# Twenty row sums moved behind the dense tiles' picks in a hybrid layer with product-key experts

## The chip, the cores and the metric

The kernel runs on one core of one Trainium2 chip, in float32. The metric is device time in microseconds of one execution; lower is better. "Before" has a median of 1618.62 us over three runs (1617.82 to 1620.2).

## What is computed

One layer over 512 tokens of width 1024: a token-mixing sublayer (windowed attention and an HGRN2 recurrence, merged by gates, projected, layer norm) and then the part that this case is about, a PEER layer that picks 16 experts of 16384 for each of 8 heads and each token:

```python
def block(xt):                                   # 128 tokens
    q = (xt @ wq).reshape(128, 8, 2, 128)
    s1 = einsum('thd,kd->thk', q[:, :, 0], keys[0]);  s2 = ... keys[1]
    v1, i1 = top_k(s1, 16);  v2, i2 = top_k(s2, 16)
    cand = v1[..., :, None] + v2[..., None, :]   # 256 sums
    sc, ci = top_k(cand, 16)
    e = i1[ci // 16] * 128 + i2[ci % 16]         # expert number
    g = softmax(sc)
    act = gelu(einsum('thkd,td->thk', u[e], xt))
    return einsum('thk,thkd->td', g * act, v[e])
x = layer_norm(ALPHA * x + mix(x));  x = layer_norm(ALPHA * x + peer(x))
```

`u` is the first table and `v` the second, 16384 rows of 1024 each.

## The kernel before

The tokens are four tiles of 128. Tile 0 goes through the mixing sublayer alone (`A`), tiles 1 to 3 together (`B`). Then PEER is done in two ways.

**Tiles 0 and 1 gather.** For each of the 128 picks (8 heads x 16) of a token tile, GpSimd fetches 128 rows of 4 KB (0.524 MB) by an indirect DMA into one of 12 slots, and VectorE handles this "row": for `u` a product with x summed up (L1181), for `v` a scaled addition to the result (L1196). There are 512 such rows: 0 to 127 are `u` for tile 0, 128 to 255 `v` for tile 0, 256 to 383 `u` for tile 1, 384 to 511 `v` for tile 1. GpSimd refills a pair of slots once VectorE has used them. A hand-written plan says how many rows VectorE has done at each place of its program (`rows_until`). VectorE's instructions run in the order written, so a row in front of a step delays the step.

**Tiles 2 and 3 are dense.** They go through both tables in whole. A first-table block c is 128 experts: TensorE multiplies a `u` block of 0.524 MB with both tiles (L855, 16 records), ScalarE applies gelu, `act[c]` stays on chip or is spilled to `act_d`. There are 128 such blocks and TensorE starts them as soon as `B` is projected. Four `u` buffers: SyncE asks for block c's when block c - 4 is done. Meanwhile VectorE routes tile 1 (four pairs of heads) and tiles 2 and 3 (two halves each), with rows between the steps. Then come the "picks": normalised gates and expert halves, turned by TensorE (L864), copied by ScalarE. In between, at block `TURN_AT`, TensorE waits for them (`pick_ready`). From them VectorE makes 64 one-hot pairs (`one_hots`, L1504 and L1506), with `HOT_ROWS` rows spread over them, and TensorE multiplies each pair (`spread`, four matrix products, L873), which gives the gates of four tokens for all 16384 experts, a "gate product" below. `quads_by` says after which block which one is due. ScalarE copies them, and six groups of eight go to memory (`gates_d`); the last two stay on chip.

In the second table, block i of `act` is multiplied by its gates on VectorE (`weigh`, L1521 and L1522), which waits for its slice of eight blocks of gates (`load_gates`), and TensorE adds its product with a `v` block (`combine`, L879, 8 records). VectorE's remaining rows are spread over this table by `rows_at`, then tile 1's norm. At the very end the norms of tiles 2 and 3 follow.

SyncE issues nearly all loads in one order, waiting as written. Before, after the last `u` load:

```python
            sp.wait_ge(pick_ready, len(DENSE))
            for i in range(2):
                load_v(i)
            for k in range(2):
                sp.wait_ge(g_stored[k], 16 * (STORED // 2))
            load_gates(0)
            sp.wait_ge(g_done, QUADS)
```

The second slice, `load_gates(1)`, takes the place of the first table's input and so is asked for after the last block of it.

Of the kernel before, what the change touches and what calls it, by code (L numbers as in the profile page):

```python
# [36 lines left out]
NE = PH * TOPK  # L37
# [25 lines left out]
DENSE = (2, 3)  # L63
ND = len(DENSE) * P
EXPERTS = NK
# [3 lines left out]
FIRST = SPILL + RINGED_ACT  # L69
# [4 lines left out]
STORED = GROUPS - 2  # L74
# [1 line left out]
QUADS = ND // QUAD  # L76
GBLK = 8
EXP1_AT = 24
EXP_AT = 50
TURN_AT = 52  # L80
SPREAD_AT, SPREAD_END = 53, 116
ROOT0_Q = 44
GELU1_AT = 112
PAIR = 2
EARLY_ROWS, PAIR_ROWS, HALF_ROWS = 204, 7, 8
HOT_ROWS = 104
MID_ROWS = 390
ACT_BACK_LEAD = 12


# [9 lines left out]

def rows_at(i):

    return min(4 * NE, MID_ROWS + int(3.2 * min(i, EXPERTS - FIRST)) + int(1.0 * max(0, i - EXPERTS + FIRST)))


NORM1_W = min(i for i in range(EXPERTS) if rows_at(i) == 4 * NE)
# [77 lines left out]
def build(nc, x, xT, w_items, keysT, pos, inv_freq, sinks, lb_logits, norm_g,  # L184
          ln1, ln2, ident_d, causal_d, chunk_d, iota_d, u_rows, v_rows, u_cols, v_cols, gates_d, act_d, out):
    with ExitStack() as ctx:
# [253 lines left out]
        def _(sp):  # L440
# [54 lines left out]
            def load_v(i):  # L495

                if i >= VBUFS:
                    sp.wait_ge(o_done, i - VBUFS + 1)
                sp.dma_start(v_buf[i % VBUFS], v_cols[chunk(i)]).then_inc(v_in[i % VBUFS], 16)

            def load_gates(b):

                if b >= 2:
                    sp.wait_ge(w_ready, GBLK * (b - 1))
                src = gates_d.rearrange("g p (b n) -> b p g n", b=EXPERTS // GBLK)
                sp.dma_start(g_buf[b % 2].rearrange("p g c t -> p g (c t)"), src[chunk(b * GBLK) // GBLK]
                             ).then_inc(g_in[b % 2], 16)
# [19 lines left out]
            for c in range(EXPERTS):  # L527
                load_u(c)
                b, late = divmod(c - BATCH - UBUFS, BATCH)
                if late == 0 and 0 <= b < SPILL // BATCH:  # L530
                    spill(b)
            sp.wait_ge(pick_ready, len(DENSE))
            for i in range(2):
                load_v(i)
            for k in range(2):
                sp.wait_ge(g_stored[k], 16 * (STORED // 2))
            load_gates(0)
            sp.wait_ge(g_done, QUADS)
            for i in range(2, 4):
                load_v(i)  # L540
# [591 lines left out]
        def _(dve):  # L1132
# [38 lines left out]
            def rows_until(q):  # L1171

                while done[0] < q:
                    r = done[0]
                    s, t, k = r % SLOTS, r // (2 * NE), r % NE
                    if r % (2 * NE) < NE:
                        if t and k == NE // 2:
                            dve.wait_ge(row_used, r)
                            dve.sem_inc(hid_ready, 1)
                        dve.wait_ge(landed[s // 2], 32 * (r // SLOTS + 1))  # L1180
                        v.tensor_tensor_reduce(rows[:, s, :], rows[:, s, :], x1[:, t, :], 1.0, 0.0,  # L1181
                                               ALU.mult, ALU.add, hid[:, k:k + 1]).then_inc(row_used, 1)
                    else:
                        if k == 0:
                            dve.wait_ge(row_used, r)
                            dve.sem_inc(hid_ready, 1)
                            dve.wait_ge(gexp_done, t + 1)
                            normalise(gexp)
                            weights(t + 1, slice(0, NE // 2 if t else NE))
                            steps(lambda: v.tensor_scalar(acc[t], x1[:, t, :], ALPHA, None, ALU.mult))  # L1190
                        if t and k == NE // 2:
                            weights(t + 2, slice(NE // 2, NE))
                        dve.wait_ge(landed[s // 2], 32 * (r // SLOTS + 1))

                        dve.wait_ge(row_used, r)
                        v.scalar_tensor_tensor(out=acc[t], in0=rows[:, s, :], scalar=wv[:, k:k + 1], in1=acc[t],  # L1196
                                               op0=ALU.mult, op1=ALU.add).then_inc(row_used, 1)
                    done[0] += 1
# [296 lines left out]
            def one_hots(d, first):  # L1495

                dve.wait_ge(pick_out, 2 * (d + 1))
                for q in range(d * QUADS // len(DENSE), (d + 1) * QUADS // len(DENSE)):
                    if q >= 2:
                        dve.wait_ge(g_done, q - 1)  # L1500
                    ts = slice(q * QUAD - d * P, (q + 1) * QUAD - d * P)
                    both = [P, 2, QUAD, NK]
                    out = hot[:, q % 2, :, :].rearrange("p (k j) e -> p k j e", k=2)
                    steps(lambda: v.tensor_tensor(out, iota[:, :].unsqueeze(1).unsqueeze(1).to_broadcast(both),  # L1504
                                                  idxT[d][:, :, ts].unsqueeze(3).to_broadcast(both), ALU.is_equal))
                    v.tensor_tensor(out[:, 1, :, :], out[:, 1, :, :],  # L1506
                                    gT[d][:, ts].unsqueeze(2).to_broadcast([P, QUAD, NK]), ALU.mult).then_inc(hot_ready, 1)
                    rows_until(first + HOT_ROWS * (q + 1) // QUADS)

# [74 lines left out]
                gate_args(d)  # L1584
            for d in range(len(DENSE)):
                gate_weights(d)
            rows_until(2 * NE)
            dve.wait_ge(row_used, 2 * NE)
            dve.wait_ge(ln_in, 64)
            dve.sem_inc(route_gate, 1)  # L1590
            one_hots(0, first)
            both_stats(acc[0])
            one_hots(1, first)
            norm_scale(0, acc[0], std2_ready, y2_ready)
# [89 lines left out]
```

## Time and profile before

| | us |
|---|---|
| Median of three runs | 1618.62 |
| Profiled execution | 1628.27 |
| Its span | 1626.5 |
| TensorE (PE) busy | 1540.3, 95% |
| VectorE (DVE) busy | 1130.7, 70% |
| GpSimd (POOL) busy | 623.7, 38% |
| ScalarE (ACT) busy | 273.8, 17% |
| Mixing and projections, TensorE | 0 to 650.0 |
| First table, TensorE | 652.8 to 1168.3 |
| Second table, TensorE | 1177.1 to 1619.2 |

The queues moved 532.39 MB, 327 GB/s over the span. A float32 matrix product stands in the trace as two records. Times in the trace are of the profiled execution, which is 9.65 us longer than the median of the others.

### The profile page before, as it was taken

How to read it: one execution, taken by the hardware profiler on the slowest of the kernel's cores; microseconds unless marked ns; L12 is line 12 of the kernel's file. 1: busy time of each engine (PE TensorE's matmuls, PEld its weight loads, DVE VectorE, ACT ScalarE, POOL GpSimd, SP SyncE). 2: the span in 40 equal slices, each digit the busy share in tenths (PEclk: the TensorE clock that was granted, in tenths of full speed). 3: DMA queues.
4: the chain of work that ended last, by engine and by line, in shares of the span. 5: the costliest groups of instructions: out<-in, count | busy, mean ns of one | idle time of the engine just before them, and what ended most of it. 6: DMA issues, size and time to landing. Idle time of an engine off the chain costs nothing.

```text
span 1626.5 us, 18100 instructions
## 1 busy us (share of the span) xinstructions
PE 1540.3 (95%) x6542; PEld 1098.4 (68%) x6542; DVE 1130.7 (70%) x2492; ACT 273.8 (17%) x543; POOL 623.7 (38%) x516
## 2 busy tenths in 40 slices
PE   7798799869999899999979999999799999999998
PEld 7697568755557666888869999999644444444443
DVE  1413889877778989999998888889574544444442
ACT  2601111731010112111113333433100000000000
POOL 0001533455676473323225555555543323323200
PEclk9898899878999999999989999999999999999999
DMA  7586958757999898998879999999999999999952
GB/s 290 208 280 220 401 167 298 258 191 243 414 388 374 309 413 332 320 344 302 328 250 338 405 415 411 405 381 324 392 403 392 381 374 369 376 371 376 363 199 90
DMA packets 142856, 532.39 MB, mean 327 GB/s; under 512 B 15024, under 2 KB 30128, under 8 KB 130480
## 3 DMA queue, kind: packets, MB, share of 16 engines
q0 software_dynamic: 73728, 268.47, 44.2%
q1 hardware_dynamic: 68176, 250.19, 41.0%
q10 hardware_dynamic: 864, 12.58, 1.8%
q8 instruction: 52, 0.85, 0.2%
q14 instruction: 36, 0.29, 0.0%
HBM read 503.92 MB, written 27.26 MB: 327 GB/s over the span
## 4 chain that ended last, share of the span: by engine, by line
PE 71%; DVE 15%; issue 6%; DMA 3%; ACT 2%; POOL 1%; SPq 1%; another core or an unknown queue 0%; DVEq 0%
PE bank L879 27%; PE bank L855 15%; PE bank L749 7%; PE bank L596 4%; PE bank L873 4%; DVE arena L1196 3%; PE bank L584 3%; DVE arena L1401 2%; PE bank L835 2%; DVE arena L1397 2%; PE bank L759 2%; PE bank L761 2%; POOL arena L1619 1%; PE bank L780 1%; DVE arena L1406 1%
## 5 line engine op out<-in xcount | busy, mean ns | idle before, releaser
L1619 POOL DMA_INDIRECT arena<-u_d,arena x256 | 341.6, 1334 | 496.9 <-DVE arena L1181 253.8
L855 PE MATMUL bank<-arena 128*128 128x256 f32 x2048 | 456.8, 381 | 2.7 <-DMA arena<-u_cols_d 2.7
L879 PE MATMUL bank<-arena 128*128 128x512 f32 x1024 | 442.1, 595 | 8.8 <-DVE arena L1522 8.8
L1619 POOL DMA_INDIRECT arena<-v_d,arena x256 | 281.9, 1101 | 404.9 <-DVE arena L1196 345.3
L855 PEld LDWEIGHTS bank<-arena 128*128 128x128 f32 x2048 | 387.0, 192 | 53.6 <-issue 2.9
L879 PEld LDWEIGHTS bank<-arena 128*128 128x128 f32 x1024 | 195.4, 191 | 255.0 <-issue 243.9
L1196 DVE SCALAR_TENSOR_TENSOR arena<-arena 128x1024 f32<-128x1024 f32 x256 | 327.5, 1279 | 13.0 <-DMA arena<-v_d,arena 3.6
L1181 DVE CUSTOM_DVE_ANT_0 arena<-arena 128x1024 f32<-128x1024 f32 x256 | 303.2, 1219 | 12.1 <-DMA arena<-u_d,arena 11.7
L1521 DVE TENSOR_TENSOR arena<-arena 128x192 f32<-128x192 f32 x128 | 45.0, 352 | 208.3 <-DMA arena<-act_d 167.4
L835 PE MATMUL bank<-arena 128*128 128x128 f32 (+1 forms) x512 | 124.0, 401 | 9.7 <-issue 7.8
L835 PEld LDWEIGHTS bank<-arena 128*128 128x128 f32 x512 | 84.8, 208 | 45.6 <-issue 12.0
L749 PE MATMUL bank<-arena 128*128 128x128 f32 (+1 forms) x512 | 114.4, 385 | 0.0
L1074 ACT ACTIVATE arena<-bank 128x256 f32<-128x256 f32 x128 | 49.0, 384 | 343.0 <-PE bank L855 332.0
L749 PEld LDWEIGHTS bank<-arena 128*128 128x128 f32 x512 | 78.3, 193 | 35.0 <-issue 2.0
L596 PE MATMUL bank<-arena 128*128 128x256 f32 x448 | 98.7, 383 | 0.0
L596 PEld LDWEIGHTS bank<-arena 128*128 128x128 f32 x448 | 85.7, 192 | 12.3 <-issue 0.2
L1102 ACT ACTIVATE rstd<-rstd 128x1 f32<-128x1 f32 x4 | 0.8, 202 | 450.7 <-DVE rstd L1377 450.6
L1093 ACT ACTIVATE arena<-bank 128x512 f32<-128x512 f32 x64 | 69.1, 1082 | 31.5 <-PE bank L873 28.4
L873 PEld LDWEIGHTS bank<-arena 128*128 128x128 f32 x512 | 67.1, 192 | 3.3
L873 PE MATMUL bank<-arena 128*128 128x128 f32 x512 | 67.3, 275 | 0.0
L584 PE MATMUL bank<-arena 128*128 128x128 f32 (+1 forms) x256 | 57.9, 390 | 8.5 <-DMA arena<-w_items_d 8.5
L584 PEld LDWEIGHTS bank<-arena 128*128 128x128 f32 x256 | 40.4, 200 | 25.4 <-issue 7.5
(199 smaller groups left out, 1115.7 us busy)
## 6 DMA issues: line engine op xcount, KB each, us to landing
arena<-w_items_d SPq DMA_DIRECT2D x66, 1024.0 KB, 8.7
arena<-u_cols_d SPq DMA_DIRECT2D x128, 512.0 KB
arena<-v_cols_d SPq DMA_DIRECT2D x128, 512.0 KB
act_d<-arena SPq DMA_DIRECT2D x12, 1024.0 KB, 10.3
gates_d<-arena ACTq DMA_DIRECT2D x6, 2048.0 KB
arena<-gates_d SPq DMA_DIRECT2D x16, 768.0 KB, 10.1
arena<-act_d SPq DMA_DIRECT2D x12, 1024.0 KB, 12.3
arena<-u_d,arena POOLq DMA_INDIRECT x256
```

The costliest lines, as they stand in the source:

```text
L584: last = mm(bank[:, b % 4, 0:n], w[:, c, b % 2 * P:(b % 2 + 1) * P], F.act_in[:, c, :], start=c == 0, stop=c == KC - 1)
L596: last = mm(bank[:, b % 4, 0:TW], F.act_in[:, c, t * P:(t + 1) * P], w[:, c, :], start=c == 0, stop=c == KC - 1)
L749: last = mm(bank[:, b + g, 0:n], w[:, g * KC + c, :], F.act_in[:, c, :], start=c == 0, stop=c == KC - 1)
L835: last = mm(bank[:, b % 4, 0:n], w[:, c, half * P:(half + 1) * P], F.act_in[:, c, :], start=c == 0, stop=c == KC - 1)
L855: last = mm(bank[:, 4 + c % 2, 0:ND], u_buf[:, c % UBUFS, k, :], B.act_in[:, k, B.n - ND:B.n], start=k == 0, stop=k == KC - 1)
L873: last = mm(bank[:, 6 + q % 2, j * NK:(j + 1) * NK], hot[:, q % 2, j, :], hot[:, q % 2, QUAD + j, :], start=True, stop=True)
L879: return mm(bank[:, 2 * n + half, :], act_slot(i)[:, n * P:(n + 1) * P], v_buf[i % VBUFS][:, half * 512:(half + 1) * 512], start=i == 0, s ...
L1074: fn(act_ring[c % RINGED_ACT], bank[:, 4 + c % 2, 0:ND], ACT.Gelu).then_inc(act_done, 1)
L1093: fn(stage[g % 2][:, :, k * QUAD:(k + 1) * QUAD].rearrange("p e t -> p t e"), bank[:, 6 + q % 2, :].rearrange("p (t e) -> p t e", t=QUAD), ...
L1181: v.tensor_tensor_reduce(rows[:, s, :], rows[:, s, :], x1[:, t, :], 1.0, 0.0, ALU.mult, ALU.add, hid[:, k:k + 1]).then_inc(row_used, 1)
L1196: v.scalar_tensor_tensor(out=acc[t], in0=rows[:, s, :], scalar=wv[:, k:k + 1], in1=acc[t], op0=ALU.mult, op1=ALU.add).then_inc(row_used, 1)
L1619: pool.indirect_dma_start(rows[:, r % SLOTS, :], None, table, bass.IndirectOffsetOnAxis(eidx[:, t, k:k + 1], 0)).then_inc(landed[r % SLOTS ...
```

## The change

Six numbers of the plan, two places in SyncE's order and one in VectorE's.

```diff
-EXP_AT = 50
-TURN_AT = 52
-SPREAD_AT, SPREAD_END = 53, 116
+EXP_AT = 44
+TURN_AT = 46
+SPREAD_AT, SPREAD_END = 47, 118
+GATES_AT, VALUES_AT = 114, 118
-EARLY_ROWS, PAIR_ROWS, HALF_ROWS = 204, 7, 8
-HOT_ROWS = 104
-MID_ROWS = 390
+EARLY_ROWS, PAIR_ROWS, HALF_ROWS = 192, 6, 7
+HOT_ROWS = 126
+MID_ROWS = 374
 ...
-    return min(4 * NE, MID_ROWS + int(3.2 * min(i, EXPERTS - FIRST)) + int(1.0 * max(0, i - EXPERTS + FIRST)))
+    return min(4 * NE, MID_ROWS + int(3.2 * min(i, EXPERTS - FIRST)) + int(1.1 * max(0, i - EXPERTS + FIRST)))
 ...
                     spill(b)
-            sp.wait_ge(pick_ready, len(DENSE))
-            for i in range(2):
-                load_v(i)
-            for k in range(2):
-                sp.wait_ge(g_stored[k], 16 * (STORED // 2))
-            load_gates(0)
+                if c == GATES_AT:
+                    sp.wait_ge(pick_ready, len(DENSE))
+                    for k in range(2):
+                        sp.wait_ge(g_stored[k], 16 * (STORED // 2))
+                    load_gates(0)
+                if c == VALUES_AT:
+                    for i in range(2):
+                        load_v(i)
             sp.wait_ge(g_done, QUADS)
 ...
                 gate_weights(d)
-            rows_until(2 * NE)
+            one_hots(0, first)
+            assert done[0] >= 2 * NE
             dve.wait_ge(row_used, 2 * NE)
             dve.wait_ge(ln_in, 64)
             dve.sem_inc(route_gate, 1)
-            one_hots(0, first)
             both_stats(acc[0])
```

Rows done at each place, worked out from these numbers:

| Place in VectorE's program | before | after |
|---|---|---|
| start of tile 1's routing | 204 | 192 |
| after tile 1's four pairs | 232 | 216 |
| after the four halves, at the picks | 264 | 244 |
| after the 64 one-hot pairs | 368 | 370 |
| before block 0 is weighed | 390 | 374 |
| all 512, at block | 122 | 126 |

(SPREAD_AT and SPREAD_END give the blocks: 64 gate products over 63 blocks before, over 71 after.) With 244 rows at the picks, tile 0 (256 rows) is not finished there, so the wait for its last row moves behind the first 32 one-hot pairs, just ahead of its statistics.

What stands in a row on VectorE between the end of `B`'s norms and the first steps of tile 1's routing (L1196 is a value row, L1397 the first maximum of the routing), before:

```order
L1384 RECIPROCAL rstd<-rstd 128x1
L1387 SCALAR_TENSOR_TENSOR arena<-arena,rstd 128x512 x2
L1196 SCALAR_TENSOR_TENSOR arena<-arena 128x1024 x44
L1397 MAX arena<-arena 128x8 x4
L1401 MAX_INDEX arena<-arena 128x8 x4
L1406 MATCH_REPLACE arena<-arena 128x128 x4
```

and after (lines are three further down):

```order
L1387 RECIPROCAL rstd<-rstd 128x1
L1390 SCALAR_TENSOR_TENSOR arena<-arena,rstd 128x512 x2
L1199 SCALAR_TENSOR_TENSOR arena<-arena 128x1024 x32
L1400 MAX arena<-arena 128x8 x4
L1404 MAX_INDEX arena<-arena 128x8 x4
L1409 MATCH_REPLACE arena<-arena 128x128 x4
```

Twelve value rows have left this place.

TensorE from the last key scores over the first-table blocks (eight matrix products each) to the picks and the first gate products, before:

```order
L823 MATMUL bank<-keys,arena 128x128 x12
L855 MATMUL bank<-arena 128x256 x416
L864 MATMUL bank<-ident,arena 128x128 x3
L864 MATMUL bank<-ident,state_in 128x128 x2
L864 MATMUL bank<-ident,arena 128x128
L855 MATMUL bank<-arena 128x256 x16
L873 MATMUL bank<-arena 128x128 x4
L855 MATMUL bank<-arena 128x256 x8
```

and after:

```order
L826 MATMUL bank<-keys,arena 128x128 x12
L858 MATMUL bank<-arena 128x256 x368
L867 MATMUL bank<-ident,arena 128x128 x3
L867 MATMUL bank<-ident,state_in 128x128 x2
L867 MATMUL bank<-ident,arena 128x128
L858 MATMUL bank<-arena 128x256 x24
L876 MATMUL bank<-arena 128x128 x4
L858 MATMUL bank<-arena 128x256 x8
```

The picks stand after 46 blocks instead of 52, and three blocks instead of two lie between them and the first gate product.

SyncE's queue from the last spill (`act_d`) to the second gate slice, before:

```order
L514 DMA act_d<-arena 128x2048
L492 DMA arena<-u_cols_d 128x1024 x27
L499 DMA arena<-v_cols_d 128x1024 x2
L506 DMA arena<-gates_d 128x6x256
L499 DMA arena<-v_cols_d 128x1024 x6
L506 DMA arena<-gates_d 128x6x256
```

and after:

```order
L515 DMA act_d<-arena 128x2048
L493 DMA arena<-u_cols_d 128x1024 x14
L507 DMA arena<-gates_d 128x6x256
L493 DMA arena<-u_cols_d 128x1024 x4
L500 DMA arena<-v_cols_d 128x1024 x2
L493 DMA arena<-u_cols_d 128x1024 x9
L500 DMA arena<-v_cols_d 128x1024 x6
L507 DMA arena<-gates_d 128x6x256
```

The first slice stands ahead of the last thirteen `u` loads and the first two `v` blocks ahead of the last nine.

## Rows read from the trace of the kernel before

**Rows 1.** Page, part 1: busy us (share) xinstructions:

```profile
PE 1540.3 (95%) x6542; PEld 1098.4 (68%) x6542; DVE 1130.7 (70%) x2492; ACT 273.8 (17%) x543; POOL 623.7 (38%) x516
```

**Rows 2.** Timeline of PE at the first table; start us, us, line, xcount, [idle before]:

```profile
652.75 12.50 PE L855 MATMUL bank<-arena 128*128 128x256 f32 x49 [2.73 <-DMA arena<-u_cols_d]
...
809.70 24.55 PE L855 MATMUL bank<-arena 128*128 128x256 f32 x113
844.57 0.90 PE L864 MATMUL bank<-ident,arena 128*128 128x128 f32 x3 [10.32 <-DVEq L1493]
...
846.27 9.30 PE L855 MATMUL bank<-arena 128*128 128x256 f32 x32
855.40 1.05 PE L873 MATMUL bank<-arena 128*128 128x128 f32 x8
...
859.75 1.05 PE L873 MATMUL bank<-arena 128*128 128x128 f32 x8
```

**Rows 3.** Timeline of PE at the start of the second table:

```profile
1177.09 23.22 PE L879 MATMUL bank<-arena 128*128 128x512 f32 x48 [8.80 <-DVE arena L1522]
```

**Rows 4.** Stretches: us; busy (xcount) of PE, PEld, DVE, ACT, POOL; PEclk; DMA share; GB/s:

```profile
652.00:656.00 4.00, 3.25 (x8) 2.65 (x9) 3.51 (x9) 0.00 (x0) 1.51 (x3) 0.60 0.96 341
844.00:850.00 6.00, 5.33 (x15) 4.22 (x16) 4.68 (x10) 2.98 (x8) 1.64 (x2) 0.50 0.54 176
1177.00:1183.00 6.00, 5.91 (x9) 2.59 (x10) 6.00 (x13) 0.00 (x0) 2.19 (x2) 0.60 1.02 408
```

**Rows 5.** Timeline of DVE from the last norm to routing's pair 0:

```profile
552.09 44.34 DVE L1196 SCALAR_TENSOR_TENSOR arena<-arena 128x1024 f32<-128x1024 f32 x32
...
615.61 0.86 DVE L1397 MAX8 arena<-arena 128x8 f32<-128x128 f32 x4
...
636.92 1.28 DVE L1196 SCALAR_TENSOR_TENSOR arena<-arena 128x1024 f32<-128x1024 f32 x1
638.12 0.17 DVE L1572 CAST arena<-arena 128x32 uint32<-128x32 f32 x1
```

**Rows 6.** Timeline of ACT, head 3's scores copied:

```profile
618.21 0.38 ACT L1054 ACTIVATE arena<-bank 128x256 f32<-128x256 f32 x1 [0.28 <-remote]
```

**Rows 7.** Timeline of DVE, first step of tile 2's routing and tile 3's gate argument:

```profile
706.95 1.65 DVE L1397 MAX8 arena<-arena 128x8 f32<-128x128 f32 x8
...
843.41 0.29 DVE L1486 TENSOR_TENSOR arena<-arena 128x128 f32<-128x128 f32 x1
```

**Rows 8.** Timeline of DVE, one gate product with two row sums:

```profile
1121.64 1.22 DVE L1504 TENSOR_TENSOR arena<-iota,state_in 128x1024 f32<-128x1024 f32 x1
...
1123.51 1.22 DVE L1181 CUSTOM_DVE_ANT_0 arena<-arena 128x1024 f32<-128x1024 f32 x1
...
1125.80 1.28 DVE L1381 SCALAR_TENSOR_TENSOR arena<-arena,mv 128x1024 f32<-128x1024 f32 x1
```

**Rows 9.** Busy time by stretches; then PEclk, DMA share, GB/s:

```profile
888.00:1080.00 192.00, 192.00 (x1061) 173.73 (x1060) 168.79 (x238) 67.24 (x92) 103.44 (x72) 1.00 1.02 410
1190.00:1240.00 50.00, 50.00 (x118) 22.07 (x117) 25.78 (x48) 0.00 (x0) 17.22 (x16) 1.00 1.03 402
1250.00:1500.00 250.00, 250.00 (x584) 110.70 (x583) 119.16 (x223) 0.00 (x0) 80.23 (x75) 1.00 0.99 375
```

**Rows 10.** Timeline of the SP queue at the table change:

```profile
1156.61 0.38 SPq L506 DMA_DIRECT2D arena<-gates_d  x1
```

**Rows 11.** Timeline of DVE at the table change:

```profile
1176.54 0.36 DVE L1521 TENSOR_TENSOR arena<-arena 128x192 f32<-128x192 f32 x1 [14.85 <-DMA arena<-gates_d]
```

**Rows 12.** Gate values' transfers, to and from memory:

```profile
L1097 ACTq DMA_DIRECT2D gates_d<-arena x6: 326/326/347, 888.0 to 1061.9; - x6
...
DMA to landing us min/median/max: 5.5/10.1/28.6
```

**Rows 13.** Timeline of DVE at the end:

```profile
1608.91 0.69 DVE L1536 SCALAR_TENSOR_TENSOR arena<-arena,bank 128x512 f32<-128x512 f32 x1 [34.33 <-PE bank L879]
```

**Rows 14.** Timeline of PE at the end:

```profile
1579.53 39.65 PE L879 MATMUL bank<-arena 128*128 128x512 f32 x92
```

## The prediction, made before the changed kernel was run

> **What bounds the kernel now.** I read the page's busy shares first: TensorE is busy for 95% of the span [rows 1]. So the time is TensorE's work plus its few idle places, and I looked for these in its timeline. From the first table's start to the end there are three. It waits 2.73 us for the first `u` load. It stands 10.32 us ahead of the picks, after 52 of the 128 first-table blocks [rows 2]. It stands 8.80 us between the first and the second table [rows 3]. Each also costs time afterwards: the granted clock is 0.50 in the stretch after the picks, 0.60 in the stretch after the second gap and 0.60 after the first load [rows 4], that is, partly or wholly at 1.2 instead of 2.4 GHz. After the picks, two blocks take 9.13 us (846.27 to 855.40) where two of 3.46 take 6.92, so 2.2 us are lost there; the 3.46 is 181.50 us for 52 blocks (3.49 each) less the slow start. After the second gap, 48 records, which are six second-table blocks, take 23.22 us. At 8 records a block, the 584 records of 250 us give 3.42 us a block or 20.5 for six [rows 3, 9], so 2.6 us are lost.
>
> Who ends each wait? At the picks it is VectorE: it finishes tile 3's routing at 843.41, normalises the gates behind it, and TensorE starts at 844.57 [rows 2, 7]. At the table change it is the first gate slice: SyncE asks for it at 1156.61, behind all 128 `u` loads, VectorE waits 14.85 us for it and weighs block 0 from 1176.54, TensorE starts at 1177.09 [rows 3, 10, 11].
>
> **Part 1: twenty row sums later.** Twelve are taken out ahead of tile 1's routing. VectorE has done row 191 at 552.09 + 44.34 = 596.43 and starts routing at 615.61, so the twelve occupy 19.18 us, far more than 12 x 1.28: they wait for gathers [rows 5]. Is anything else late then? Pair 0 of the routing takes 22.6 us with seven rows (615.61 to about 638.2). With six it is 21.4, as a value row here holds VectorE for 1.20 (636.92 to the start of the next step at 638.12; its 1.28 overlap that step a little). It would end at 617.8, and pair 1 needs head 3's scores, copied from 618.21 to about 618.6 [rows 6]; the longest wait there is 0.8, I take 0.6. The other eight rows stand in the four pairs (615.61 to 706.95) and the four halves (706.95 to 843.41) of the routing, one in each. They give back 8 x 1.20 = 9.6, less 0.4, because the rows now done there are all value rows (1.20) and the last ones were first-table rows (1.15) [rows 5, 7, 8]. Together 19.2 + 9.2 - 0.6 = 27.8 us, and the picks are ready at 844.57 - 27.8 = 816.8. Bounds: if the gathers, not VectorE, set the pace inside the routing too, nothing beyond the twelve comes back (about 825); if the score copies come early, 816.2.
>
> **Part 2: picks six blocks earlier.** Block 46 starts at 834.25 - 6 x 3.46 = 813.5, so TensorE now waits 3.3 us instead of 10.32. ScalarE's exponentials move by the same six blocks and keep their distance. The clock still falls, I assume: after the 2.73 us wait its stretch too had 0.60 [rows 4]. I keep the picks at their 1.70 us and the 2.2 lost. Then 82 blocks are left instead of 76, with the same 64 gate products: 322.02 + 6 x 3.46 = 342.8 us, from 816.8 + 1.7 = 818.5 to 1161.3. Before, it was 1168.29. **Gain 7.0 us.** With no clock loss it is 9 or 10, with picks at 825 it would be a loss of 1.
>
> **Part 3: slower spreading, faster row sums.** 64 products now lie over 71 blocks and the first follows block 48. A block with a product is 4.35 us long [rows 2], so one product takes 0.89 and the mean spacing is (71 x 3.46 + 57) / 64 = 4.73 us against 4.30. VectorE builds a product in 1.87 us and adds rows at 1.15: two rows make 4.16 us, with the step to the next about 4.3 [rows 8]. With 126 instead of 104 rows nearly every product has two. That fits under 4.35 by little and under the mean 4.73 by 0.4, like before (3.9 under 4.30), and two buffers carry it over a run. Cost 0. Without that cover each 0.1 us a product costs 6.4 us.
>
> **Part 4: the first gate slice and the values.** SyncE asks for the slice after `u` block 114, which is after TensorE's block 110. It first waits for the stores; the last store was issued at 1061.9, after block 100, where the new plan has it too, and no transfer of gate values took over 28.6 us to land [rows 12]. The ten blocks up to block 110, of about 4.3 us, cover that, so it costs 0. The 0.79 MB of the slice and 1.05 MB of values in front of nine `u` loads are at 400 GB/s [rows 9] 2 and 2.6 us of transfer, spread over three or more blocks of lead: 0, at worst one wait of 3 us plus 2. The products end after block 117, about 35 us before the end of the first table. Then only four rows stand ahead of block 0's weighting, where six value rows and sixteen others stood. So w of block 0 is there some 25 us early: the 8.80 gap and the 2.6 of clock go. **Gain 11.4 us.** What is late next there is the second slice. It is still asked for when the first table ends, and is needed eight blocks (27.4 us) later.
>
> **Part 5: sixteen rows move into the second table.** 138 rows over 127 blocks instead of 122. VectorE waits there a good deal: it was through with its last weighting at 1608.91 - 34.33 = 1574.58, and the last four blocks' sums, which want it, start about 4 x 3.42 us before TensorE's end at 1619.18, at 1605.5 [rows 13, 14]. The last row and tile 1's norm come four blocks later now (some 14 us), which these 31 us cover. The queues carry 375 GB/s in that stretch and gain 16 x 0.524 MB / 440 us = 19 GB/s: 394, under the 402 seen at its start [rows 9]. Cost 0.
>
> **Sum.** 7.0 + 11.4 = 18.4 us of the profiled execution, which took 1628.27 (span 1626.5): 1609.9. The median of the plain runs is 1618.62, 9.65 less; the same gain gives **1600.2 us**, a ratio of 0.989.
>
> **The transfer rate** is the weak place. While products are spread, a 4.73 us spacing now moves 1.97 rows (1.032 MB), 1.11 `u` blocks (0.582), a share of spills (0.145) and of gate stores (0.262): 2.02 MB, or 428 GB/s. Before it was 1.77 MB in 4.35, 407, and the trace has 410 over 192 us with every engine of the queues busy (share 1.02), 402 in another such stretch [rows 9]. So 428 will not be reached. The 48 products up to the last store need 97 MB; twelve row slots are filled ahead (6.3 MB), and the remaining 91 MB fit in 48 x 4.73 = 227 us from 400 GB/s upward. By the rows it just fits. The Trainium skill (DMA: Bandwidth & Descriptors, Where 436 GB/s comes from) gives 435 GB/s as the ceiling, by which 428 would pass without a queue; the measured 402 to 410 at full share speak against it, and the sum is made from them. The same page (Queues, rings and completion order) has each transfer engine take turns between queues packet by packet; by that the gathers would fall behind and not the `u` loads. No row here separates the two.
>
> **Rivals.**
> - The second slice takes the longest landing seen, 28.6 us, and TensorE waits 1 to 2 us at block 8, with 2.6 of clock: 1604. Against it: few gathers run at that moment, since VectorE has stopped. Likewise one wait on a `u` load near block 119: 1605. Together 12%.
> - The queues give only 400 GB/s or less and the stock doesn't help, in one piece: 227 x (428/410 - 1) = 10 us more, 1610. 6%.
> - VectorE becomes the bound in the spreading, at 0.3 us a product over 4.73: 19 us, about 1619, no change. 4%.
> - **Slower:** below 400 GB/s the row sums run out of landed rows, TensorE waits for the products in a dozen or more short gaps, and each gap costs its clock too, 2.2 us as after the picks. 10 + 12 x 2.2 = 36 us more, 1636. It decides at 400 GB/s. For it: full share already now. Against: TensorE was busy for all of the 192 us at 407 demanded [rows 9], so nothing was late. 5%.
> - The forecast, 1596 to 1604, has 73%.
>
> **Range and chances.** 1596 to 1608 takes in the forecast with both clock bounds and the first rival. Faster by over 0.2% (about what a measurement of this kernel can tell from no change) 0.91: the forecast, the first rival and the second; within 0.2% 0.04, slower by over 0.2% 0.05.
>
> **What would show it.** In the changed kernel's profile: routing of tile 1 starts near 596.5; TensorE's idle time ahead of the picks is 2 to 4 us, with block 46 near 813.5; no idle time on TensorE between the tables, the first table ends near 1161; the matrix products of the second table start at full clock; VectorE waits for the second slice, not the first. Wrong would be idle time on TensorE ahead of the gate products or on `u` loads after block 46, a rate under 400 GB/s while the row sums wait for gathers, or picks later than 820.

## The result, and the profile after

Both kernels were timed on the same chip. The changed kernel takes 1604.6 us (median of 4 runs, 1601.83 to 1606.74) where the kernel before takes 1618.2 (4 runs): a ratio of 0.9909, 95% interval 0.9896 to 0.9922. That is 14.7 us by the ratio (12.6 to 16.8; the two medians are 13.6 apart), where 18.4 was forecast. The predicted 1600.2 is 4.4 us too low and the measured time lies inside the range of 1596 to 1608.

The profiled execution of after has a span of 1600.0 us, 26.5 less than that of before. Nearly half of this isn't the change: the key scores, the last matrix products ahead of the first table, end at 650.02 in before (652.75 less its wait of 2.73, [rows 2]) and at 637.60 in after (638.76 less 1.16, below). The moved rows are not the reason: two kernels of the experiments that keep all 204 early rows, a1_slice_only and b4_mid374, end the key scores at 638.14 and 641.51. The profiled execution of before was slow at the front by itself, mostly from 166 to 184, where TensorE has a row of short waits with no releaser that the trace shows, and the others have none; its 1628.27 stood 9.65 over the median. So I compare from the end of the key scores onward, where the two traces differ by 26.5 - 12.4 = 14.1 us.

Timeline of TensorE (PE) in after, from the first block to the table change; start us, us, line, xcount, [idle before]:

```profile
638.76 159.12 PE L858 MATMUL bank<-arena 128*128 128x256 f32 x736 [1.16 <-DMA arena<-u_cols_d]
805.62 0.90 PE L867 MATMUL bank<-ident,arena 128*128 128x128 f32 x3 [7.75 <-DVEq L1496]
...
807.32 12.37 PE L858 MATMUL bank<-arena 128*128 128x256 f32 x48
819.52 1.05 PE L876 MATMUL bank<-arena 128*128 128x128 f32 x8
...
872.08 3.72 PE L858 MATMUL bank<-arena 128*128 128x256 f32 x16 [0.24 <-DMA arena<-u_cols_d]
...
907.04 3.72 PE L858 MATMUL bank<-arena 128*128 128x256 f32 x16 [0.82 <-DMA arena<-u_cols_d]
...
1105.43 3.72 PE L858 MATMUL bank<-arena 128*128 128x256 f32 x16 [1.75 <-DMA arena<-u_cols_d]
```

Against [rows 2]: the wait ahead of the picks (805.62) is 7.75 us where it was 10.32 and where 3.3 was forecast. Behind it stand three short waits, each for a `u` load, 2.81 us together, that before doesn't have at all.

The groups by line of TensorE in after; busy us, mean ns | idle us before, by releaser. They say that for the whole first table no other wait exists (4.0 = 1.16 + 2.81), and that the second table has none:

```profile
L858 PE MATMUL bank<-arena 128*128 128x256 f32 x2048 | 455.2, 381 | 4.0 <-DMA arena<-u_cols_d 4.0
L882 PE MATMUL bank<-arena 128*128 128x512 f32 x1024 | 439.6, 592 | 0.0
```

Against [rows 3], the 8.80 us of idle time between the tables are gone. Timeline of VectorE (DVE) in after: block 0 of the second table is weighed at 1121.79, some 31 us before TensorE needs it, and the long wait is now for the second slice; it is weighed with TensorE two blocks into the table, against the eighth block for which it is needed. At the end VectorE still waits 24.36 us for TensorE, against 34.33 in [rows 13].

```profile
1121.79 0.35 DVE L1524 TENSOR_TENSOR arena<-arena 128x192 f32<-128x192 f32 x1
...
1159.93 0.36 DVE L1524 TENSOR_TENSOR arena<-arena 128x192 f32<-128x192 f32 x1 [26.80 <-DMA arena<-gates_d]
...
1582.48 0.69 DVE L1539 SCALAR_TENSOR_TENSOR arena<-arena,bank 128x512 f32<-128x512 f32 x1 [24.36 <-PE bank L882]
```

Busy time by stretches in after: us; busy (xcount) of PE, PEld, DVE, ACT, POOL; PEclk, DMA share, GB/s. They answer to [rows 4, 9]:

```profile
638.00:642.00 4.00, 3.24 (x15) 2.92 (x16) 3.71 (x13) 1.30 (x2) 0.93 (x1) 1.00 1.02 414
806.00:810.00 4.00, 3.91 (x13) 2.97 (x12) 2.89 (x5) 2.06 (x7) 0.94 (x1) 0.50 0.79 241
1153.00:1159.00 6.00, 6.00 (x16) 2.75 (x15) 0.00 (x0) 0.38 (x1) 0.00 (x0) 1.00 0.86 291
888.00:1080.00 192.00, 191.18 (x1040) 172.62 (x1040) 167.99 (x243) 63.14 (x88) 113.44 (x80) 1.00 1.02 414
1085.00:1110.00 25.00, 23.25 (x131) 20.97 (x131) 22.26 (x34) 7.73 (x12) 18.99 (x13) 1.00 1.03 404
1250.00:1500.00 250.00, 250.00 (x584) 110.83 (x583) 126.82 (x229) 0.00 (x0) 89.62 (x81) 1.00 1.01 385
```

The granted clock at the second table's start is full (2.4 GHz) instead of 0.60. After the picks it is 0.50 as before: the three blocks from 807.32 to 819.52 take 12.20 us instead of 3 x 3.46 = 10.38, so 1.8 us are lost there. And the clock was kept after the first wait, which is 1.16 us now, not 2.73. The queues carry 414 GB/s in the stretch that had 410.

Where the 14.1 us come from, from the end of the key scores on:

| stretch | before, us | after, us | gain |
|---|---|---|---|
| end of the key scores to the end of the first table | 518.27 | 515.51 | 2.8 |
| gap between the tables | 8.80 | 0 | 8.8 |
| second table | 442.09 | 439.63 | 2.5 |

The second and third lines are the 11.4 us of Part 4, met to 0.1. The first should have been 7.0.

### The profile page after: what moved, and what is told of

Read it like the earlier page. It is cut to its first block, busy times and chain, and to the rows that moved or that the text cites. A ratio compares the mean times of both kernels' runs of the same rounds, so it can differ in the third digit from the quotient of the medians.

```text
span 1600.0 us, 18099 instructions
## 1 busy us (share of the span) xinstructions
PE 1527.8 (95%) x6542; PEld 1090.2 (68%) x6542; DVE 1130.7 (71%) x2492; ACT 274.0 (17%) x543; POOL 621.9 (39%) x516
## 4 chain that ended last, share of the span: by engine, by line
PE 63%; DVE 23%; issue 6%; DMA 5%; ACT 2%; POOL 0%; DVEq 0%; SPq 0%
PE bank L882 27%; PE bank L858 16%; PE bank L752 7%; DVE arena L1199 5%; DVE arena L1404 3%; PE bank L876 3%; DMA arena<-u_cols_d 3%; DVE arena L1400 2%; DVE arena L1184 2%; PE bank L762 2%; PE bank L764 2%; DVE arena L1409 2%; PE bank L783 1%; DVE arena L1441 1%; DMA arena<-u_d,arena 1%
## 5 line engine op out<-in xcount | busy, mean ns | idle before, releaser
L882 PE MATMUL bank<-arena 128*128 128x512 f32 x1024 | 439.6, 592 | 0.0
L838 PE MATMUL bank<-arena 128*128 128x128 f32 (+1 forms) x512 | 116.7, 389 | 1.4 <-ACT arena L1044 1.4
L752 PE MATMUL bank<-arena 128*128 128x128 f32 (+1 forms) x512 | 113.8, 384 | 0.0
L599 PEld LDWEIGHTS bank<-arena 128*128 128x128 f32 x448 | 86.3, 193 | 15.6 <-ACT arena L936 3.3
L587 PE MATMUL bank<-arena 128*128 128x128 f32 (+1 forms) x256 | 58.6, 395 | 7.3 <-DMA arena<-w_items_d 7.3
```

The costliest lines, as they stand in the source:

```text
L587: last = mm(bank[:, b % 4, 0:n], w[:, c, b % 2 * P:(b % 2 + 1) * P], F.act_in[:, c, :], start=c == 0, stop=c == KC - 1)
L599: last = mm(bank[:, b % 4, 0:TW], F.act_in[:, c, t * P:(t + 1) * P], w[:, c, :], start=c == 0, stop=c == KC - 1)
L752: last = mm(bank[:, b + g, 0:n], w[:, g * KC + c, :], F.act_in[:, c, :], start=c == 0, stop=c == KC - 1)
L838: last = mm(bank[:, b % 4, 0:n], w[:, c, half * P:(half + 1) * P], F.act_in[:, c, :], start=c == 0, stop=c == KC - 1)
L882: return mm(bank[:, 2 * n + half, :], act_slot(i)[:, n * P:(n + 1) * P], v_buf[i % VBUFS][:, half * 512:(half + 1) * 512], start=i == 0, s ...
```

## The experiments

I had two questions. What ended the gap: the place of the first slice in SyncE's order, as Part 4 has it, or the row sums? And where did 4.2 us of the first table go? All ratios are against the kernel before on the same chip.

**The slice alone**, the kernel before with only SyncE's new order (the lines in brackets stand for code that the change above shows in full):

```
+GATES_AT, VALUES_AT = 114, 118
 ROOT0_Q = 44
 ...
+                if c == GATES_AT:
+                    (waits of picks and stores, load_gates(0))
+                if c == VALUES_AT:
+                    (load_v(0), load_v(1))
-            (the same, behind the loop)
```

> The kernel before with one part of the change: the first gate slice is asked for after u block 114 and the first two v blocks after u block 118; rows, picks and gate products stay as they were. Theory A (the gap between the tables comes from the place of the slice in SyncE's queue): no idle time of TensorE between the tables, the picks' wait stays at about 10 us, and the gain is 8.8 + 2.6 = 11.4 us, a ratio of 0.993. Theory B (the gap comes from the gathers that 22 rows ahead of the second table set off): the slice lands late or a v or u block does, a gap of 2 us or more stays, gain 3 to 8 us, ratio 0.995 to 0.998. The u load right behind the slice should wait as in the changed kernel (1 to 2 us) if the slice in front of it is its cause.

Measured: 1606.87 us, ratio 0.9935 (0.9921 to 0.9949), so 10.5 us. No gap: the second table starts at 1157.00 right behind the first. The picks' wait is 10.80. No wait follows the slice here; the queues carry 349 GB/s at 1085 to 1110 in this kernel, since its rows are spread as before.

**The rows and picks alone**, the changed kernel with SyncE's old order, and **the changed kernel once more** beside it:

> The changed kernel with its slice and v blocks asked for at the old place, behind all u loads. Theory A: the gap between the tables comes back, 5 to 9 us, and with 2.6 us of clock; this kernel is 8 to 11 us slower than the changed one, ratio to before about 0.998. Theory B: without the 16 rows' gathers in the queues the slice lands in 8 us instead of 19.8, before the first table has ended, and there is no gap: ratio about 0.991, as the changed kernel. No wait on a u load near block 115 by either.

> The changed kernel again, for its trace and its time beside the others. If the three waits on u loads (0.24, 0.82 and 1.75 us) come from the plan, they stand again at about the same blocks; if they are chance, elsewhere or not at all. The same for the early start of the first table against the picks: TensorE's wait ahead of the picks 7 to 8 us again, ratio 0.991.

Measured: 1600.85 us, ratio 0.9894 (0.9879 to 0.991), for the rows alone; 1603.04, ratio 0.991 (0.9895 to 0.9926), for the change again. The half without the slice's move has the whole gain, 17.1 us against 14.5 (the intervals overlap). That was unexpected by my Part 4: the slice is asked for at its old place, and still there is no gap.

The repeated run also says which waits of the change come from the plan. The picks' wait (7.95 us), the wait at block 115 (1.66 us at 1106.88) and one near 907 are there again; the one at 872 is not, and there is one at 943 instead. So of the `u` waits ahead of the slice the number and the places vary from run to run. Timeline of TensorE in a3_after_again; a2_rows_only has the same two, 0.95 us at 907.61 and 0.84 at 943.49:

```profile
907.50 3.72 PE L858 MATMUL bank<-arena 128*128 128x256 f32 x16 [0.43 <-DMA arena<-u_cols_d]
...
943.35 7.17 PE L858 MATMUL bank<-arena 128*128 128x256 f32 x32 [0.82 <-DMA arena<-u_cols_d]
```

The timeline of SyncE's queue and that of VectorE in a2_rows_only:

```profile
1140.57 0.38 SPq L507 DMA_DIRECT2D arena<-gates_d  x1
```

```profile
1148.31 0.36 DVE L1522 TENSOR_TENSOR arena<-arena 128x192 f32<-128x192 f32 x1 [26.77 <-DMA arena<-gates_d]
```

The slice is used 7.7 us after it was asked for. In before it took 19.9 (1156.61 to 1176.54, [rows 10, 11]). What lies beside it is different. In before, 22 rows stand between the last product and block 0's weighting, and GpSimd issues their gathers up to 1166; here four stand there, the last gather is issued at 1123.98, and from 1128 to 1148 the queues run at a share of 0.78:

```profile
1128.00:1148.00 20.00, 20.00 (x94) 17.63 (x93) 0.00 (x0) 2.30 (x6) 0.00 (x0) 1.00 0.78 272
```

**The moved rows alone, without the picks and without the slice's place.** To make sure, the kernel before with 16 rows given to the second table, and no other edit:

```
-MID_ROWS = 390
+MID_ROWS = 374
-    ... + int(1.0 * max(0, i - EXPERTS + FIRST)))
+    ... + int(1.1 * max(0, i - EXPERTS + FIRST)))
```

> The kernel before with only 374 instead of 390 rows ahead of the second table and 1.1 instead of 1.0 a block in it; picks, products and SyncE's order as before. Theory B (the first slice took 19.8 us because of the gathers of the 22 rows that VectorE takes at a run before it): the run is 6 rows, the slice lands in 8 to 10 us, before the first table has ended or 1 us behind it, the gap goes with its clock: gain 9 to 11.4 us, ratio 0.993 to 0.9945. Theory A (the slice's place): the gap stays at 6 us or more, ratio over 0.997.

Measured: 1607.9 us, ratio 0.9933 (0.992 to 0.9947), 10.8 us. No gap (the second table starts at 1160.49 without idle time), with the slice asked for at 1148.25 and VectorE at block 0 from 1155.59, 7.3 us later. So each of the two edits removes the whole gap by itself, 10.5 and 10.8 us, and together they bring no more than one.

**Are the full queues the cause of the new waits?** The changed kernel with 22 rows fewer in the spreading, given to the second table:

```
-HOT_ROWS = 126
-MID_ROWS = 374
+HOT_ROWS = 104
+MID_ROWS = 352
-    ... + int(1.1 * ...
+    ... + int(1.27 * ...
```

> The changed kernel with 104 instead of 126 rows between the gate products; the 22 rows move into the second table (352 rows ahead of it, 1.27 a block). Theory (the queues are at their limit while gates are stored, so u loads land late): demand there falls from 428 to 390 GB/s, no wait on a u load at the blocks of 872 and 907 us, first table 1 to 3 us shorter; but the second table wants 412 GB/s, so v blocks or act may be waited for. Rival (the waits on u are single accidents or come from the slice alone): the one behind the slice stays, the time is that of the changed kernel within 1 us, or slower by what the second table loses.

Measured: 1602.74 us, ratio 0.9909 (0.9896 to 0.9923). At 1085 to 1110 the queues carry 327 GB/s at a share of 0.96, and TensorE is busy for all 25 us: the wait behind the slice is gone. But the two earlier ones stay, 0.67 us at 874.59 and 1.28 at 910.02. In their stretch, 852 to 912, the queues carry 384 GB/s here and 413 in after. So the rate is one half of the cause of the wait at 1105. The first two outlast a rate lower by 7%; with the share still at 0.99 this run can't say what emptier queues would do to them.

**Are the first two the spills'?** SyncE writes a 1 MB piece of hidden activations out every eight blocks, and ScalarE stores gate values, 2 MB at a time, every nine products. In before every store leaves 19.0 us behind a spill (869.06 and 888.04 are the first such pair), since both come every 34.77 us. With the picks six blocks earlier and the products spread wider, the stores moved against the spills, which count `u` blocks. Timeline of SyncE's queue in after, the spills being L515, and of TensorE as above:

```profile
854.91 1.08 SPq L515 DMA_DIRECT2D act_d<-arena  x1
858.83 30.37 SPq L493 DMA_DIRECT2D arena<-u_cols_d  x8
889.30 0.38 SPq L515 DMA_DIRECT2D act_d<-arena  x1
893.22 30.95 SPq L493 DMA_DIRECT2D arena<-u_cols_d  x8
```

The first two stores are issued at 852.15 and 890.88, so within 2.8 us of the spills at 854.91 and 889.30. Each of these has a `u` load as the next transfer of its queue, asked for at 858.83 and 893.22, and TensorE waits until 872.08 and 907.04. The four later pairs are 5.9 us and more apart, and nothing waits. The experiment moves the spills four blocks later:

```
-                b, late = divmod(c - BATCH - UBUFS, BATCH)
+                b, late = divmod(c - BATCH - UBUFS - 4, BATCH)
```

> The changed kernel with every spill of act asked for four blocks later. Theory (a u load lands late when it stands behind a 1 MB spill in SyncE's queue while a 2 MB gate store is under way; in the changed kernel spills and stores start within 6 us of each other for the first three stores): the waits at about 907 and 943 us go, and such waits come at the fifth or sixth store, near 1015 to 1050 us, where spill and store now meet. Rival (they come from the load of the queues alone): the waits stay at 907 and 943. The wait of 1.7 us behind the slice stays by both.

Measured: 1603.54 us (2 runs), ratio 0.9909 (0.9891 to 0.9927), no different from the change. But the trace answers: all waits near 872, 907 and 943 are gone, and one comes where the shifted spill (1045.03) and the sixth store (1046.60) now meet. The one near 907 counts most, since every other trace with the change's picks has it; the one at 872 comes and goes by itself. Timeline of TensorE in b2_spills4, all its waits behind the picks:

```profile
1063.12 3.72 PE L858 MATMUL bank<-arena 128*128 128x256 f32 x16 [0.28 <-DMA arena<-u_cols_d]
...
1107.78 3.72 PE L858 MATMUL bank<-arena 128*128 128x256 f32 x16 [1.82 <-DMA arena<-u_cols_d]
```

The 0.8 us that this saves is too little to be seen in the time; it is the places of the waits that speak. They do so in all twelve traces together. Behind the picks, apart from those right behind the slice, TensorE waited thirteen times for a `u` load, always 17 to 19 us behind a spill that stood near a store:

| store issued after its spill by | pairs | followed by a wait | us |
|---|---|---|---|
| -2.8 us (the store first) | 7 | 3 | 0.24 to 0.68 |
| 1.6 us | 7 | 7 | 0.28 to 1.28 |
| 5.9 us | 6 | 3 | 0.82 to 0.96 |
| 7 us and more apart, either way | all others, the kernel before's among them | 0 | |

A store is not the only company that makes a `u` load late, though. Ahead of the picks, where there are no stores, five traces have one more such wait each, of 0.18 to 1.60 us and 13.5 to 15 us behind a spill. That is four blocks of 3.46, as the 17 to 19 are four of about 4.35: TensorE waits for the load that was asked for right behind the spill in both cases. The longest is in b4_mid374, behind the spill of 677.61; from 677 to 693 the queues carry 343 GB/s at a share of 0.95. No run moved this one, and most spills there have no wait behind them.

```profile
692.62 7.61 PE L855 MATMUL bank<-arena 128*128 128x256 f32 x34 [1.60 <-DMA arena<-u_cols_d]
```

**Is the wait at 1105 the slice's?** Timeline of SyncE's queue in after: the slice (L507), four `u` loads, the two values (L500):

```profile
1085.87 0.38 SPq L507 DMA_DIRECT2D arena<-gates_d  x1
1089.78 13.37 SPq L493 DMA_DIRECT2D arena<-u_cols_d  x4
1103.19 0.91 SPq L500 DMA_DIRECT2D arena<-v_cols_d  x2
```

The `u` load asked for at 1089.78, block 115's, right behind the slice, took 15.6 us to land, and TensorE starts at 1105.43; the median of the 128 is 6.8. SyncE's loads of 1085 to 1100 in after, as that stretch's view of the line gives them, and in a2_rows_only, which has no slice there:

```profile
DMA to landing us min/median/max: 8.3/12.9/15.6
```

```profile
DMA to landing us min/median/max: 6.7/7.5/8.0
```

The experiment asks for the slice eight blocks later:

```
-GATES_AT, VALUES_AT = 114, 118
+GATES_AT, VALUES_AT = 122, 124
```

> The changed kernel with the slice behind u block 122 and the first two v blocks behind 124 instead of 114 and 118. Theory (block 115's u load lands late because it stands right behind the slice while the gathers catch up, 404 GB/s up to 1110 us): no wait on a u load near there, no gap between the tables, time as a2's, 0.9894, 2 us under the changed kernel's. Rival (what a2 gained over the changed kernel is scatter): 0.991.

Measured: 1602.17 us, ratio 0.9896 (0.9881 to 0.9911). There is no wait near it (slice asked for at 1124.72, TensorE busy for 25.00 of the 25 us from 1085 at 410 GB/s) and still no gap. The time agrees with a2_rows_only (0.9894) and is a little under the change (0.9909, 0.991), though the intervals overlap. So the slice's early place costs one wait of 1.7 us where the queues are full behind it, and brings nothing in return here.

**What are the picks worth that don't wait at all?** In after TensorE still stands 7.75 us ahead of them. The picks three blocks later again, on a2_rows_only:

```
-EXP_AT = 44
-TURN_AT = 46
-SPREAD_AT, SPREAD_END = 47, 118
+EXP_AT = 47
+TURN_AT = 49
+SPREAD_AT, SPREAD_END = 50, 121
```

> The changed rows with slice and v blocks at the old place (a2), and the picks three blocks later: TURN_AT 49, products over 72 blocks from 50 to 121. Theory (TensorE stood 7.3 to 8 us ahead of the picks, because it reached block 46 earlier than forecast; three blocks are 10.4 us): no wait ahead of the picks, the clock stays up, and the first table ends 7.3 + 0.8 + 1.8 = 10 us earlier than in a2; gate stores start 8 us or more after the spills, so the waits on u behind a spill (0.95 and 0.84 us) go too. Ratio to before about 0.983. Rival (VectorE's products or the queues set the pace now): TensorE waits elsewhere, ahead of the products or on u, and the time stays within 3 us of a2's, 0.989.

Measured: **1590.5 us**, ratio 0.9828 (0.9814 to 0.9841), 27.8 us under the kernel before, 10.7 under a2_rows_only and some 13 under the change (by the ratios). Timeline of TensorE in b1_picks49:

```profile
789.76 21.53 PE L856 MATMUL bank<-arena 128*128 128x256 f32 x99
811.13 0.49 PE L865 MATMUL bank<-ident,arena 128*128 128x128 f32 x3
...
811.79 10.53 PE L856 MATMUL bank<-arena 128*128 128x256 f32 x48
822.15 1.05 PE L874 MATMUL bank<-arena 128*128 128x128 f32 x8
...
1141.78 23.77 PE L880 MATMUL bank<-arena 128*128 128x512 f32 x55
```

No idle time stands ahead of the picks; they take 0.66 us (811.13 to 811.79) instead of 1.70, and three blocks take 10.36 behind them instead of 12.20. From the end of the key scores (640.99 less a wait of 1.16) to the second table it is 501.95 us instead of 515.51, 13.6 less. I can name 12.9 of them: 7.75 of wait, 1.0 in the picks, 1.8 of clock, 2.8 of `u` waits gone, less one new wait of 0.58 at 769.59. No spill is within 7 us of a store now (844.50 and 854.78 are the first pair), and TensorE waits for no `u` load after the picks. The granted clock is full in every 4 us from 804 to 828:

```profile
808.00:812.00 4.00, 4.00 (x23) 3.54 (x22) 0.52 (x3) 1.53 (x5) 0.94 (x1) 1.00 0.89 280
812.00:816.00 4.00, 4.00 (x20) 3.53 (x19) 3.72 (x4) 1.04 (x5) 0.00 (x0) 1.00 0.95 347
```

**Two more ask what of this version depends on what.** First, the same with the slice among the `u` loads, behind block 117's, and the values behind 121's (its expectation says "before"):

> b1_picks49 once more, but with SyncE's order of the changed kernel: the first gate slice asked for among the u loads (before block 117's, three later than in the changed kernel because the picks are three blocks later), the values before block 121's. My theory: the slice's place brings nothing once the row sums are moved, and costs one wait of TensorE for the u load right behind it, 1.7 to 1.8 us as in after, a3_after_again and b2_spills4. So a wait of 1 to 2 us on a u load near 1100 us, no gap between the tables, and about 1592 us (ratio 0.983 to 0.985). Rival: in b3_slice122 a later place had no such wait, so at 117 it may be gone as well: then 1590.5, the same as b1_picks49. If it is faster than 1589, the early slice has a worth of its own that I have missed.

Measured: 1590.91 us, ratio 0.9836 (0.9819 to 0.9852), the same as b1_picks49. My 1.7 us were too much: the wait behind the slice is 0.30 us (at 1104.85), at the same 404 GB/s. The load behind the slice lands in 14.2 us at most here, where it took 15.6 in after. So even with full queues the early slice doesn't always cost; why that load is 1.4 us quicker here stays open.

Second, the picks put back to block 52, where the kernel before has them:

> b1_picks49 with the picks put back where the kernel before has them, after block 52 (exponentials at 50, products over 53 to 124): the row sums of the change, none of its earlier picks, SyncE's old order. It tells whether the earlier picks of the change are worth anything by themselves. My theory: what costs time is only TensorE's idle time ahead of the picks and the clock lost behind it; the picks are ready near 805 to 809 us, TensorE is through with block 52 near 822, so nothing waits, as in b1_picks49: 1590 to 1592 us, ratio 0.982 to 0.984. Rival: the six blocks matter for what comes behind. The products end after block 123, the last store and the first slice come later, and the gap between the tables or a wait of 1 to 3 us on u loads comes back: 1593 to 1600 us.

Measured: 1595.62 us, ratio 0.9869 (0.9852 to 0.9886). The rival was right. The picks don't wait, but the gap comes back, and two `u` waits with it, 0.93 us at 992.35 and 0.96 at 1027.45. With 1.8 us of clock in the second table (441.4 us for it, 439.6 in b1_picks49) these make up 7.7 of the 7.8 us that this trace loses to that of b1_picks49 from the end of the key scores on; by the ratios it is 6.6. Timelines of TensorE, of SyncE's queue and of VectorE in c2_picks52 at the table change:

```profile
1143.79 26.79 PE L880 MATMUL bank<-arena 128*128 128x512 f32 x58 [4.08 <-DVE arena L1523]
```

```profile
1126.49 0.40 SPq L507 DMA_DIRECT2D arena<-gates_d  x1
```

```profile
1143.24 0.36 DVE L1522 TENSOR_TENSOR arena<-arena 128x192 f32<-128x192 f32 x1 [14.21 <-DMA arena<-gates_d]
```

The slice took 16.7 us here. The products end three blocks later than in b1_picks49, so the last gathers too: they are issued up to 1131.49, after the slice was asked for (1126.49). Five kernels with the slice behind all `u` loads now line up:

| kernel | slice asked for | last gather issued | asked to used |
|---|---|---|---|
| before | 1156.61 | 1165.29 | 19.9 |
| c2_picks52 | 1126.49 | 1131.49 | 16.7 |
| b1_picks49 | 1130.39 | 1123.35 | 8.9 |
| a2_rows_only | 1140.57 | 1123.98 | 7.7 |
| b4_mid374 | 1148.25 | 1131.78 | 7.3 |

Where gathers are still being issued when the slice is asked for, it takes 17 to 20 us; where they ended 7 us or more earlier, 7 to 9. So the six blocks by which the picks went forward have a worth that I had not seen: with the products spread over 71 blocks, they end them, and with them the gathers, before the slice. By the table it is that end which counts and not the picks' place: b4_mid374 has its picks after block 52 too, but its products end after block 115, and it has no gap.

## Why the prediction was right, and where it was off

**The direction and the range** were right, by the steps that carry most of it. Part 4's number (8.80 us of gap and 2.6 of clock) came as 8.80 and 2.46. Part 5 is right: the second table takes 439.63 us with no idle time, at 385 GB/s (394 was expected), and VectorE's slack at the end shrank by 10 us of 34, which cost nothing. Part 3 is right in its sum: VectorE keeps up with two rows a product, and no gate product is waited for.

**Part 4's reason was incomplete.** "So w of block 0 is there some 25 us early: the 8.80 gap and the 2.6 of clock go" gives the gain to the slice's new place. a1_slice_only shows that the place does it, but a2_rows_only and b4_mid374 show that the rows alone do it too. I had the fact in Part 4 ("where six value rows and sixteen others stood") and counted it only as work of VectorE. It is transfer as well, and it lay in front of the slice. The sum was saved by counting the gap once. The same part's "0, at worst one wait of 3 us plus 2" should have been the wait: 1.75 us of TensorE, with no loss of clock.

**Part 2 is the mis-sized term**: 7.0 forecast, 2.8 measured. Three things make the 4.2:

- The picks are ready 1.2 us late: at 805.62, where Part 1's 816.8 less the 12.4 us of the slow front is 804.4. Part 1 is good otherwise: tile 1's routing starts at 584.56, or 597.0 on the clock of before, for the forecast 596.5.
- The three `u` waits, 2.81 us, were priced at 0 or left to a rival. The rival "one wait on a `u` load near block 119" names the one at 1105, which came at block 115. The two at 872 and 907 are in no step: the diff doesn't move the spills, and I didn't ask what the stores' move towards them would do. Part 2 should have written both series down, spills and stores, before and after.
- The clock and the rest come to 0.2: 1.8 instead of 2.2 us lost after the picks, 0.6 elsewhere that I can't assign.

The wait itself, 7.75 for 3.3, looks like the largest miss, but only the 1.2 us above cost time: 3.2 of the 4.5 us are TensorE's arrival, which is that much earlier. Its first wait is 1.6 us shorter and the clock behind it was kept. While VectorE sets the picks' time, that arrival is worth nothing. It is worth something as soon as the picks stand later, and that is what b1_picks49 takes: 7.75 us of wait, the clock and the slower picks, 10.6 us together.

**The transfer rate**: "428 will not be reached" holds, 414 GB/s were. TensorE never waited for a product. VectorE did wait, 4.3 us in three places after the picks, within its slack. On who falls behind the text went wrong. The Trainium skill (DMA: Bandwidth & Descriptors, Queues, rings and completion order) says that transfer engines switch between queues packet by packet; I took from it that the gathers would fall behind and not the `u` loads. Both did, and only the `u` loads cost time. What I left out is the order within a queue: the late loads stood behind a spill or a slice in SyncE's own queue, while a store or the gathers were under way on the others. Turns between the queues would make such a load late; that is an argument, as no trace here shows the turns.

**A step without a run**: why the first `u` wait is shorter. It is 2.73, 2.96 and 2.69 us in the three kernels with 204 early rows (before, a1_slice_only, b4_mid374), and 0.93 to 1.22 in the nine with 192, so it goes with that edit. Fewer gathers beside the first loads would explain it. No run moved the early rows alone.

## What to carry to other kernels

When an edit moves a point in one engine's program, list everything that counts from that point and everything that doesn't: here the gate stores moved and the spills stayed, and their meeting cost what no step of the sum had. A late transfer has two remedies, asking earlier and clearing what is in front of it; price one after the other, for they don't add up. And when a wait is shortened from both sides, look once more at where it should stand: the last three blocks of shift were worth 10.7 us (0.9894 to 0.9828), where the whole change had brought 14.7.

## What the runs showed of the hardware

- The granted clock behind a wait went with the wait's length, after TensorE had been busy at 1.00. Behind the first `u` wait of 2.73, 2.96 and 2.69 us it was 0.57 to 0.60 over 4 us; behind the first waits of the other nine traces, 0.93 to 1.22 us, it was 1.00. Nor did it fall behind the 0.82 and 1.75 us at 907 and 1105 in after, or the 1.60 us in b4_mid374. Behind the gap of 4.08 us in c2_picks52 it was 0.59, behind the picks' wait of 7.75 us 0.50.
- A load of 0.5 MB that took 6.8 us in the median took 15.6 directly behind one of 0.79 MB in the same queue, with all queues full (share 1.03, 404 GB/s). With the queues at 327 GB/s it took 7.3 at most (a4_hot104, 1085 to 1100). In c1_picks49_slice it took 14.2 at most and cost TensorE only 0.30 us at the same 404 GB/s; what differs there stays open.
- The same 0.79 MB load took from 7.3 to 19.9 us from request to use, the long times where gathers were still being issued when it was asked for (table above). b4_mid374 against before, which differ in 16 rows, is the experiment on it; the others agree.
- The highest rate over 192 us was 414 GB/s, at a share of 1.02, in after and in six of its variants, among them b1_picks49, in which TensorE waited for nothing in those 192 us.
